# Passages into and between the last two layers split by token pairs, with the context pair's norm and first four weight units placed beside the latent pair's chain

## The reference, cut to what matters

```python
def second_block(x, c, ctx, c_ctx, ...):
    xc = ctx
    for l in range(DEPTH_2):                       # two layers
        shift, scale, gate = split(silu(c) @ w_ada[l] + b_ada[l])
        shift_c, scale_c, gate_c = split(silu(c_ctx) @ w_ada[l] + b_ada[l])
        h_lat = rms_norm(x, norm_g[l]) * (1.0 + scale) + shift
        h_ctx = rms_norm(xc, norm_g[l]) * (1.0 + scale_c) + shift_c
        # projections h @ w_in[l], two attentions, gates
        x = x + gate * (... @ w_out[l])
        if l < DEPTH_2 - 1:
            xc = xc + gate_c * (... @ w_out[l])
    return rms_norm(x, final_g)
```

## Time and profile before

| | |
|---|---|
| device time, three runs | 2981.06, 2983.63, 2983.66 us (median 2983.63) |
| profiled execution | 2983.62 us, its span 2981.8 us |
| TensorE busy | 2867.1 us, 96% of the span |
| VectorE, ScalarE, GpSimd busy | 2049.0, 1243.8, 145.2 us |
| mean granted TensorE clock | 0.989 of 2.4 GHz |
| DMA | 589.44 MB, mean 198 GB/s |

### The profile page before, as it was taken

One profiled execution on the slowest core, in us unless ns is written; L12 is line 12 of the kernel. 1 busy time (PEld: TensorE's weight loads), 2 busy tenths in 40 slices (PEclk: granted clock), 3 DMA queues, 4 the chain that ended last, 5 costly groups with the idle time before them and its releaser, 6 DMA issues.

```text
span 2981.8 us, 38127 instructions
## 1 busy us (share of the span) xinstructions
PE 2867.1 (96%) x14307; PEld 2344.2 (79%) x14307; DVE 2049.0 (69%) x2919; ACT 1243.8 (42%) x2120; POOL 145.2 (5%) x225
## 2 busy tenths in 40 slices
PE   6999999998999999999999999999999999999998
PEld 2587667988778888887887888887878887888886
DVE  3368745837778889997895848873457686775466
ACT  3322525517345455454344332324445224445353
POOL 1100000001010000000000100000001001001000
PEclk9999999999999999999999999999999999999999
DMA  9877044841768777787886545772214564775334
GB/s 364 306 267 241 25 136 154 279 168 36 274 203 266 253 255 251 250 265 250 283 289 206 184 131 167 239 228 69 75 57 153 204 212 130 239 267 156 105 126 146
DMA packets 282822, 589.44 MB, mean 198 GB/s; under 512 B 31073, under 2 KB 64073, under 8 KB 278928
## 3 DMA queue, kind: packets, MB, share of 16 engines
q1 hardware_dynamic: 272240, 546.64, 56.0%
q0 software_dynamic: 10000, 39.72, 3.8%
q10 hardware_dynamic: 400, 0.66, 0.1%
HBM read 572.21 MB, written 14.72 MB: 197 GB/s over the span
## 4 chain that ended last, share of the span: by engine, by line
PE 75%; DVE 7%; ACT 3%; issue 2%; DMA 1%; POOL 0%; DVEq 0%; ACTq 0%; POOLq 0%
PE bank L3299 19%; PE bank L3301 19%; PE bank L3300 19%; PE bank L3309 2%; PE bank L3311 2%; PE bank L3310 2%; PE bank L1423 2%; DVE acc L739 2%; DVE w_lo L3236 1%; PE bank L1414 1%; ACT w_hi L3206 1%; PE bank L2453 1%; PE bank L883 1%; PE bank L1126 0%; PE bank L999 0%
## 5 line engine op out<-in xcount | busy, mean ns | idle before, releaser
L3236 DVE TENSOR_TENSOR w_lo<-raw,w_hi 128x1024 fp32r<-128x1024 f32 (+2 forms) x668 | 785.4, 1187 | 435.5 <-ACT w_hi L3206 428.0
L3206 ACT ACTIVATE w_hi<-raw 128x1024 fp32r<-128x1024 f32 (+2 forms) x668 | 679.6, 1031 | 913.9 <-PE bank L3301 639.1
L739 DVE SCALAR_TENSOR_TENSOR acc<-raw,sc_t,acc 128x1024 f32<-128x1024 f32 x480 | 601.3, 1280 | 23.6 <-DMA acc<-in_b_ada 18.7
L3299 PE MATMUL bank<-w_hi,l_hT_hi 128*128 128x512 f32 (+1 forms) x1056 | 390.2, 370 | 7.0 <-DVE w_lo L3236 4.8
L3301 PE MATMUL bank<-w_hi,l_hT_lo 128*128 128x512 f32 (+1 forms) x1056 | 387.6, 367 | 0.0
L3300 PE MATMUL bank<-w_lo,l_hT_hi 128*128 128x512 f32 (+1 forms) x1056 | 387.4, 367 | 0.0
L3299 PE MATMUL bank<-w_hi,f_hT_hi 128*128 128x512 f32 x704 | 278.1, 395 | 1.4 <-DVE mod L787 1.1
L3301 PE MATMUL bank<-w_hi,f_hT_lo 128*128 128x512 f32 x704 | 275.0, 391 | 0.0
L3300 PE MATMUL bank<-w_lo,f_hT_hi 128*128 128x512 f32 x704 | 274.8, 390 | 0.0
L3299 PEld LDWEIGHTS bank<-w_hi,l_hT_hi 128*128 128x128 f32 x1056 | 198.8, 188 | 43.7 <-DVE w_lo L3236 6.8
L3301 PEld LDWEIGHTS bank<-w_hi,l_hT_lo 128*128 128x128 f32 x1056 | 198.9, 188 | 31.5
(11 more groups left out here) (480 smaller groups left out, 4618.6 us busy)
## 6 DMA issues: line engine op xcount, KB each, us to landing
raw<-in_w_in SPq DMA_DIRECT2D x240, 512.0 KB, 4.8
raw<-in_w_mod SPq DMA_DIRECT2D x192, 512.0 KB, 5.3
raw<-in_w_ada SPq DMA_DIRECT2D x192, 512.0 KB, 4.5
raw<-in_w_up SPq DMA_DIRECT2D x176, 512.0 KB, 4.7
raw<-in_w_out SPq DMA_DIRECT2D x96, 512.0 KB, 4.9
raw<-in_w_down SPq DMA_DIRECT2D x88, 512.0 KB, 5.4
raw<-in_w_in SPq DMA_DIRECT2D x32, 288.0 KB, 3.2
raw<-in_w_ukv SPq DMA_DIRECT2D x32, 256.0 KB, 3.3
```

The costliest lines, as they stand in the source:

```text
L739: e.scalar_tensor_tensor(acc[a][:, :], raw[s % RAW_SLOTS][:, :], scalar, acc[a][:, :], ALU.mult, ALU.add).then_inc(fma_done, 1)
L3206: e.activation(slot(w_hi[u % SPLIT_SLOTS], g.width), slot(raw[s % RAW_SLOTS], g.width), ACT.Copy).then_inc(hi_ready, 1)
L3236: e.tensor_tensor(slot(w_lo[u % SPLIT_SLOTS], g.width), slot(raw[s % RAW_SLOTS], g.width), slot(w_hi[u % SPLIT_SLOTS], g.width).bitcast(F3 ...
L3299: e.matmul(o, xh[:, k, tok], hi[:, kk, :], start=first, stop=False)
```

## The change

For each passage a new function takes the place of `norm_join`: `into_layers` (A) and `between_layers` (B), both built on `norm_sets`. The tokens are taken as two sets, context tiles (2, 3) and latent tiles (0, 1). The first four q are done for one set after the other, and the first four weight units (`head = 4`) are multiplied for the context set and then again from the same `w_hi`/`w_lo` buffers for the latent set (`pe_head`); a unit counts as used only after its latent part. From q = 4 on it goes by all four tiles as before. In B the last four units of the last `w_out` group are cut in the same way (`pe_tail`). The spins are gone. The sum's 32 matmuls stand before unit 15 of the last down group in A and between the two parts of the tail in B. The context squares of A move from units 18 and 20 to 15 and 17. The scale of the norm and the context tiles' `rsqrt` are hooked before VectorE's split of unit 20. The queues of VectorE and ScalarE through the passages are written out by hand. In A `l0_hT` is placed as two halves, and the squares of the last down group go to SBUF. In these queues `turn(i)`, `affine(e, i)`, `split(e, i)` and `z(e, i)` mean item i: 0 to 3 are q = 0 to 3 of the context set, 4 to 7 of the latent set, 8 to 11 are q = 4 to 7 of all tiles.

```diff
+        def norm_sets(group0, X, sets, nt, bufs, ring, tmp, hi, lo, gain, v_shift, v_scale, late, bank_at, head=4):
+
+            n = n_seen.setdefault("set", {"k": 0, "dve": 0, "act": 0})
+            scales = n_seen["scale"] = n_seen.get("scale", 0) + 1
+            kb = n["k"]
...
+            items = [(q, s) for s in range(len(sets)) for q in range(head)] + [(q, None) for q in range(head, KT // 2)]
...
+                who = "act" if s is not None and q >= 2 else "dve"
...
+            def turn_pe(i):
+                def pe(e):
+                    who, count = makers[i]
+                    e.wait_ge(set_rows[who], count)
+                    for kk in range(2):
+                        b = spots[i][kk]
+                        users = [2 * m + k2 for m in range(i) for k2 in range(2) if spots[m][k2] == b]
+                        if users:
+                            e.wait_ge(set_aff, kb + users[-1] + 1)
+                        for n_ in range(len(tiles_of(i))):
+                            mm = e.transpose(banks[b][:, P * n_:P * n_ + P], zs[i][:, n_, P * kk:P * kk + P], ident)
+                        mm.then_inc(set_tr, 1)
+                return pe
...
+            def affine(e, i):
+                q = items[i][0]
+                e.wait_ge(norm_scale, scales)
+                for kk in range(2):
+                    p, k = 2 * i + kk, 2 * q + kk
+                    b = spots[i][kk]
+                    e.wait_ge(set_tr, kb + p + 1)
+                    if p >= 4:
+                        e.wait_ge(set_split, kb + p - 3)
+                    tiles = tiles_of(i)
+                    for pair in range(2):
+                        mine = [t for t in tiles if t // 2 == pair]
+                        if mine:
+                            at = P * tiles.index(mine[0])
+                            last = e.activation(tmp[:, p % 4, P * mine[0]:P * mine[-1] + P], banks[b][:, at:at + P * len(mine)], ACT.Identity,
+                                                bias=modv[:, v_shift, k, pair:pair + 1], scale=modv[:, v_scale, k, pair:pair + 1])
+                    last.then_inc(set_aff, 1)
...
-                yield "act", at(gs_down[3], ctx_free + 7), ctx_squares(0)
-                yield "act", at(gs_down[3], ctx_free + 9), ctx_squares(1)
+                yield "act", at(gs_down[3], 15), ctx_squares(0)
+                yield "act", at(gs_down[3], 17), ctx_squares(1)
...
+        def set_hooks(N, group0, gains):
+
+            def hooks(steps):
+                def parts(at):
+                    for n in range(6):
+                        when = at(group0, 4 + n) if n < 4 else at(group0, 7) + n - 3
+                        if n < 3:
+                            yield "pe", at(group0, 4 + n), N["turn"](9 + n)
+                        yield "act", when, lambda e, n=n: N["affine"](e, 6 + n)
+                        yield "pool", when, lambda e, n=n: N["cast"](e, 6 + n)
+                        if n < 4:
+                            yield "dve", when, lambda e, n=n: N["z"](e, 8 + n)
+                        yield "dve", when, lambda e, n=n: N["split"](e, 6 + n)
+                    yield "pool", at(group0, 7) + 2, gains
+                return join_hooks(steps, parts)
+            return hooks
...
+            def ctx_scale_dve(e):
+                N["late_scale"](e)
+                e.wait_ge(ctx_sq, 2)
+                chain(e, "dve", e.reduce_sum(tiny[:, 114:116], tiny[:, 12:20].rearrange("p (t i) -> p t i", i=4), AX_X))
+                rsqrt(e, tiny[:, 114:116], tiny[:, 58:60], tiny[:, 66:68], 1.0 / D)
+                e.sem_inc(set_rs, 1)
+
+            def ctx_dve(e):
+                z(e, 0)
+                z(e, 1)
+                split(e, 0)
+                dve_split(e, group0, 0)
+                split(e, 1)
+                dve_split(e, group0, 1)
+                split(e, 2)
+                split(e, 3)
+                dve_split(e, group0, 2)
+
+            def ctx_act(e):
+                e.wait_ge(unit_used, last.units[17] + 1)
+                e.wait_ge(set_rs, 1)
+                z(e, 2)
+                affine(e, 0)
+                z(e, 3)
+                act_split(e, group0, 0)
+                affine(e, 1)
+                act_split(e, group0, 1)
+                affine(e, 2)
+                affine(e, 3)
+                act_split(e, group0, 2)
+
+            def ctx_pool(e):
+                for i in range(4):
+                    cast(e, i)
+            hook(down.hooks, "pe", unit(15), late_pe)
+            hook(down.hooks, "dve", unit(20), ctx_scale_dve)
+            down.ahead_of_leaves["dve"].append(ctx_dve)
+            down.ahead_of_leaves["act"].append(ctx_act)
+            hook(down.hooks, "pool", len(down.steps), ctx_pool)
+            for i in range(3):
+                hook(down.hooks, "pe", unit(19 + i), turn(i))
+
+            def lat_dve(e):
+                pre2["dve"](e, lambda e: dve_split(e, group0, 3))
+                e.sem_inc(set_rs, 1)
+                z(e, 4)
+                z(e, 5)
+                split(e, 4)
+                split(e, 5)
+
+            def lat_act(e):
+                act_split(e, group0, 3)
+                pre2["act"](e)
+                e.wait_ge(set_rs, 2)
+                affine(e, 4)
+                z(e, 6)
+                affine(e, 5)
+                z(e, 7)
+
+            def lat_pool(e):
+                pre2["pool"](e)
+                cast(e, 4)
+                cast(e, 5)
...
+            group0.head_pieces.update({(0, 0): [turn(3)], (1, 0): [turn(4), turn(5)], (1, 1): [turn(6)], (1, 2): [turn(7)], (1, 3): [turn(8)]})
...
+            def dve(e, g):
+                e.wait_ge(set_out, 1)
+                residual_dve(e, 0)
+                N["late_scale"](e)
+                scale_dve(e, 0)
+                z(e, 0)
+                dve_split(e, group0, 0)
+                z(e, 1)
+                split(e, 0)
+                dve_split(e, group0, 1)
+                split(e, 1)
+                dve_split(e, group0, 2)
+                e.wait_ge(unit_used, out_group.units[-1] + 1)
+                residual_dve(e, 1)
+                e.sem_inc(evac_dve, 1)
+                split(e, 2)
+                dve_split(e, group0, 3)
+                split(e, 3)
+                scale_dve(e, 1)
+                z(e, 4)
+                z(e, 5)
+                split(e, 4)
+                split(e, 5)
+
+            def act(e, g):
+                squares_act(e, 0)
+                act_split(e, group0, 0)
+                act_split(e, group0, 1)
+                e.wait_ge(set_rs, 3)
+                z(e, 2)
+                affine(e, 0)
+                z(e, 3)
+                act_split(e, group0, 2)
+                affine(e, 1)
+                act_split(e, group0, 3)
+                affine(e, 2)
+                squares_act(e, 1)
+                e.sem_inc(evac_act, 1)
+                affine(e, 3)
+                e.wait_ge(set_rs, 4)
+                affine(e, 4)
+                z(e, 6)
+                affine(e, 5)
+                z(e, 7)
+
+            def pool(e):
+                for i in range(4):
+                    cast(e, i)
+                done["spill"](e)
+                cast(e, 4)
+                cast(e, 5)
...
+            out_group.tail_pieces[1, 7] = [turn(0)]
+            group0.head, group0.sets, group0.head_ready = 4, sets, N["ready"]
+            group0.head_pieces.update({(0, 0): [turn(1)], (0, 1): [turn(2)], (0, 2): [turn(3)], (1, 0): [turn(4), turn(5)],
+                                       (1, 1): [turn(6)], (1, 2): [turn(7)], (1, 3): [turn(8)]})
...
-            join, ready_norm = norm_join(gs[0], X, 4, z, tmp, hi, lo, V_NORM[l], 6 + 3 * l, 7 + 3 * l,
-                                         dict(pre_norm, pool=norm_pool), late, 4 if last else 7)
+            if last:
+                join, ready_norm = between_layers(gs[0], X, pre_norm, pre_pool, tmp, hi, lo, late)
+            else:
+                join, ready_norm = into_layers(gs[0], pre_pool, tmp, hi, lo, late)
...
-                  hooks=in_hooks, ready=ready_norm, prev=prev, fill=3, late=late)
+                  hooks=in_hooks, ready=ready_norm, prev=prev, late=late)
+            program[-1][2].early = gs[0].head
...
+                gs[3].tail_pieces[1, 4] = [lambda e: sums_l1[1][1].pe(e, sums_l1[1][1])]
...
         def pe_tail(e, g):
-            for t in g.tiles:
+            for s, tiles in enumerate(g.sets):
                 for j in range(g.n_units - g.tail, g.n_units):
-                    pe_unit(e, g, j, tiles=(t,))
+                    for piece in g.tail_pieces.get((s, j), ()):
+                        piece(e)
+                    pe_unit(e, g, j, tiles=tiles)
+
+        def pe_head(e, g):
+            for s, tiles in enumerate(g.sets):
+                for j in range(g.head):
+                    for piece in g.head_pieces.get((s, j), ()):
+                        piece(e)
```

(52 more changed lines are left out.)

156 lines of the change are left out of this document (126 added, 30 removed).

## The result

The changed kernel takes 2988.06 us (median of 20 runs) against 2983.77 us (20 runs): ratio 1.0014, 95% interval 1.0008 to 1.0020, so 4.3 us or 0.14% slower. The forecast was 2982.0, 1.8 us faster. Both lie within the 0.2% that counts as no change, and the time lies inside the range, but the sign is wrong, and behind it stand two passages of opposite signs.

A forecast was written before the change was run, and what follows sets the result against it. TensorE, busy 96% of the span, was taken as the bound, with at most 19.8 us to win in the two passages. A 2.1 us longer and B 3.7 shorter took 2983.62 to 2982.0 us; range 2975 to 2989.

The forecast's parts named there:

- A before T: Passage A up to the last down product (T): sum's matmuls 3.6, turns 1.5, wait 0.5, clock 1.7; +7.3 us.
- A behind T: Passage A after the last down product (T): later latent product and waits, less 10.9 of context units; -5.2 us.
- B before T: Passage B up to T: sum's matmuls 3.6 + 0.8, turn 0 0.5, low clock 1.7; +6.6 us.
- B behind T: Passage B after T: +1.0 to the latent product, less 10.9 and 0.8, plus 0.4 for restarts; -10.3 us.
- Bounds 0 and 4.3; I take 0: Passage A, unit 15's wait for context squares: tokens land about 4.5 us sooner, at 1593.4, so no wait.
- rival 3: Passage A: context load lands as late as before, unit 15 waits 4.3 us plus 1.7 of clock; 2988 us, 15%.
- The sum's matmuls: Ahead of T in both passages: 3.6 us each, 1.7 of low clock behind, 0.8 more on the matmuls in B.
- rival 2: Faster: in A no wait at unit 4 or clock loss at unit 3, clock holds behind both sums; 2974 us, 17%.
- The wait for unit 4: Passage A, TensorE waits for VectorE's work before unit 4: 2.7 us, bounds 0 and 4.5.
- rival 4: Clock falls behind every wait, 1.7 us more at the 5 us wait, unit 4 and B's waits; 2986 us, 13%.
- The clock behind the 5 us wait: Passage A, after the wait for context unit 3: low clock for part of unit 3, +0.9 us.
- The latent product: First latent product starts at T + 20.0 in A, against T + 17.54 before; at T + 14.8 in B.

The follow-up runs named there:

- ctx_early: Changed kernel with the context load issued before unit 10 of gs_down's last group, not 11: 2985.19 us, ratio 0.9996 to 1.0013 against the kernel before.
- a_fixed_look: Passage A as in `fixed`, passage B as in the kernel before, run again for an undisturbed trace: its single execution took 2980.0 us.
- hosts_late: Changed kernel with layer 0's first weight sum spread over steps 8 to 20 of w_in, not 5 to 20: 2983.53 us, ratio 0.9988 to 1.0005.
- fixed_spin: `fixed` plus five unused 512-column matmuls on TensorE in the wait before context unit 3: 2974.30 us, ratio 0.9951 to 0.9975 against the kernel before.
- order3: `fixed` with VectorE's hidden remainder of context unit 3 ahead of the residual's four additions, not behind: 2977.72 us, ratio 0.9962 to 0.9985.
- fixed: Changed kernel with four repairs: context load before unit 10, squares at 16 and 18, late sum spread, first weight sum over steps 8 to 20: 2977.32 and 2975.01 us.
- sum_spread: Changed kernel with the late sum's 16 matmuls in small groups between units in both passages, not one block: 2986.89 us, ratio 1.0003 to 1.0020.
- b_spread: New passage B alone with its late sum's matmuls spread, passage A as in the kernel before: 2977.03 us, ratio 0.9957 to 0.9982.
- a_only: Passage A as in the changed kernel, passage B as in the kernel before: 2993.35 us, ratio 1.0020 to 1.0042.
- b_only: Passage B as in the changed kernel, passage A as in the kernel before: 2980.15 us, ratio 0.9974 to 0.9991.

## Why the prediction was wrong

Its mechanism held: context units fill the latent chain's wait, and the price lies in what moves ahead of T and in what waits behind. B came out nearly as worked out. Against the terms, in the changed kernel's trace:

| | predicted | measured |
|---|---|---|
| A before T | +7.3 | +9.3 |
| A behind T | -5.2 | -2.5 |
| B before T | +6.6 | +7.3 |
| B behind T | -10.3 | -10.1 |

Measured, A before T is 1624.65 less 0.81 less the 1614.53 of the earlier trace rows; behind T is the rest of 6.9; B likewise with 2471.25 less 6.2 less 2457.73.

**The step that failed first is "Bounds 0 and 4.3; I take 0"**, for unit 15. I argued that the context tokens land 4.5 us sooner, at 1593.4, because the three `w_in` loads beside them are held back. They were held back (in the changed kernel's trace one of the three was issued between 1583 and 1602), and the tokens landed at 1596.2 to 1599.5 all the same (the traces' own shift at 1500 is 0.7 us down to 1.7 us up). In five traces with the load and its squares in these places the wait was 0.96, 2.82, 4.13, 4.23 and 4.80 us. It was rival 3's condition, which I gave 15%; ctx_early (-3.2 us) shows its price in time. That rival 3's 2988 us is the median measured is partly luck: in the profiled execution, which took 2988.45 us, the load cost 1.0 us, and most of the miss lies at unit 4.

**The sum's matmuls were undersized, in time and in clock.** The block took 4.5 us in A where I had 3.6, since the clock fell within it. Behind it the 48 products of units 15 to 18 took 12.8 us for 10.9, so 1.9 were lost where I charged 1.7; the rest of the low 6.8 us lay under the block and the wait. In B the block took 0.9 more than at the full clock, and the 36 products behind it 10.6 us for 8.2, where I had 0.8 and 1.7 for the two; spreading the block gave back 3.1. My ground for rival 2, the 1.00 of the earlier trace rows in B, says nothing of the block's price: a_fixed_look ran the same passage at 0.75 in the same 13.76 us.

**The wait for unit 4, the largest miss in this trace,** was 4.4 us, not 2.7, close to the upper bound of 4.5: a pair's `split` took 1.4 us (from 1625.71 to 1627.12, with a wait for POOL's cast in it), not 1.0, and one z over four tiles took 2.34 us. hosts_late shows that the four sum instructions on VectorE are what makes it. Behind it the clock fell for 3.2 us, 1.6 lost: this is rival 4, for which I had put nothing here.

**The clock behind the 5 us wait** was charged at 0.9; fixed_spin gives 1.3 for it. That the wait itself costs nothing was right (order3). The latent product came at T + 20.8. I had T + 20.0 and the 0.9 of clock on top of it, but the two are one: unit 3 stands ahead of turns 4 and 5, and its low clock is what holds them until 1643.41, 1.1 us after their z. So this pair of terms was right to 0.1. In B the latent product came at T + 15.4 where I had T + 14.8.

In short: in A the terms missed by 0.9 and 0.2 (sum and the clock behind it), 1.0 (load), 1.7 (unit 4) and 1.6 (clock behind it), 5.4 us, of which the trace shows 4.8 net. What gave the other 0.6 us back I did not separate. Rival 2 had no wait at unit 4 and a clock that holds behind both sums. Both come about only by repair, and then the time is near its 2974: `fixed` takes 2977.3 and 2975.0 us in its two measurements.

Where did the gain go? The kernel before did the sum's 32 matmuls inside the latent chain's wait, for nothing. The new context units need the scale that comes out of them, so they moved ahead of T in both passages, where they cost their whole length and a low clock in and behind them. Of 10.9 us of context units hidden per passage, 7 to 9 went back at once.

Of the Trainium skill's rule ("TensorE: Matmul & The Clock Gate", section "Why this matters for your kernels") that idle gaps between bursts let the clock fall: in A it held for the waits of 4.4 and 4.9 us, and fixed_spin agrees with it, while the wait of 3.48 us in the earlier trace rows kept the clock. In B the fall came with no gap at all, within a dense block of one-column matmuls.

## What to carry to other kernels

Before filling a wait with work from behind it, list what already fills it for nothing and what the new work needs first: here the same block of small matmuls (32 rows in the trace) changed from free to 4.5 us, twice. Put matmuls of one or two columns between real products a few at a time, not in a block. A load with a wait on ScalarE behind it needs to be sent as soon as its destination is free, since the splits queued behind that wait hold up TensorE; moving the wait only moves the hole. The version that pays here is both passages with the four repairs, or passage B alone with its sum spread: 0.2 to 0.4% under the kernel before. Between the two the runs do not decide.

## What the runs showed of the hardware

- The context load of 2,048 KB took 12.8 us in the kernel before, beside 3.15 MB on SP's queue between 1583 and 1602, and 12.8 us in sum_spread beside 1.39 MB; 10.4 us in the changed kernel beside 1.67 MB. Its length did not follow the traffic beside it.
- A block of 32 rows of one-column matmuls that ran back to back (16 of the program's, of which the trace shows two rows each) stands 16 times in the traces, in old and new passages. In 15 of them the granted clock fell to the lower level within the block or less than 1 us behind it, for 3.4 or 6.8 us; the one that kept it is passage B of the kernel before. In groups of 8 to 12 rows between products the clock stayed at 1.00 in all six traces of the new B with a spread sum. In the window of B shown above (2455.00:2461.80) TensorE was busy throughout at 0.54: being busy is not enough to keep the clock. The spread groups also stand earlier in the queue than the block; no run separates this from their being apart.
- Waits of 1.82 and 1.83 us at one instruction were followed by a low stretch of 3.4 us (b_spread, a_only), one of 1.80 us (b_only) was not, so single low stretches come and go between runs of near-equal code. Each of these two cost 1.6 us, which is one reason why a single trace gives a passage only to some 2 us.
